# The mixer phase of a hybrid decoder step: another order of the vector and GpSimd work between two chunks, and one buffer less

## What is computed

```
q, k = rotary(q), rotary(k)                       # retention, 4 heads
o_ret = retention(q, k, v) ; o_ret *= rsqrt(mean(o_ret^2)+eps) * ret_gn * silu(gate)
kk = kr * k_k ; kk = kk / |kk|                     # RWKV-7, 8 heads of 64
kr = kr * (1 + (a - 1) * k_a)
y, S = rwkv7_scan(r, decay, kr, vr, -kk, kk * a)
y = (y - mean) * rsqrt(var + eps) * lnx_w + lnx_b
bonus = sum(r * kr * r_k, per head) * vr
y = (y + bonus) * g
```

## Time and profile before

| | |
|---|---|
| median of 3 runs | 2093.28 us (2092.87 to 2094.78) |
| the profiled execution | 2092.87 us, span 2091.0 us, 1.9 us outside the span |
| mixer phase | from about 348 us to 790 us of the span |
| its eight pairs | from about 370 us to 734 us |
| PE busy over the span | 87% |
| mean granted PE clock | 0.929 of full speed |

### The profile page before, as it was taken

How to read it: one execution, slowest core, us unless ns; L and a number is a source line. 1 busy time by engine, 2 the same in 40 slices (tenths; PEclk the granted TensorE clock), 3 DMA queues, 4 the chain that set the end, 5 groups by cost and what they waited for, 6 DMA issues and landing times. The chain is left out here.

```text
span 2091.0 us, 35611 instructions
## 1 busy us (share of the span) xinstructions
PE 1813.1 (87%) x14874; PEld 1491.2 (71%) x14874; DVE 1191.2 (57%) x1316; ACT 825.8 (39%) x930; POOL 338.3 (16%) x307
## 2 busy tenths in 40 slices
PE   7999994888888885899999998728999999999940
PEld 7998883777777764687888885326888888888830
DVE  4543101677777565514233331167999999999916
ACT  5111211333434323402121210006777777777713
POOL 1322001234433330000000000011111111111013
PEclk9999997999999887999999999858999999999975
DMA  7765216121222208553001016249999999999837
GB/s 272 241 201 176 89 48 188 46 103 71 80 76 75 83 18 293 208 209 111 31 31 62 31 51 256 97 156 343 403 403 400 404 399 407 403 402 403 326 118 305
DMA packets 111973, 419.12 MB, mean 200 GB/s; under 512 B 25892, under 2 KB 44264, under 8 KB 82920
## 3 DMA queue, kind: packets, MB, share of 16 engines
q1 hardware_dynamic: 97272, 370.80, 47.3%
q0 software_dynamic: 7072, 25.69, 3.1%
q10 hardware_dynamic: 7504, 20.78, 2.7%
HBM read 350.10 MB, written 75.53 MB: 204 GB/s over the span
## 5 line engine op out<-in xcount | busy, mean ns | idle before, releaser
L2491 DVE TENSOR_TENSOR ex_w_lo<-moe_raw,ex_w_hi 128x2048 fp32r<-128x2048 f32 x192 | 431.2, 2284 | 67.0 <-ACT ex_w_hi L2556 66.9
L2556 ACT CAST ex_w_hi<-moe_raw 128x2048 fp32r<-128x2048 f32 x192 | 364.1, 1913 | 133.3 <-PE banks L2401 90.3
L2401 PE MATMUL banks<-ex_w_hi,ex_x_hi 128*128 128x512 f32 x512 | 208.1, 406 | 10.8 <-issue 6.3
L2401 PE MATMUL banks<-ex_w_hi,ex_x_lo 128*128 128x512 f32 x512 | 202.1, 395 | 0.0
L2401 PE MATMUL banks<-ex_w_lo,ex_x_hi 128*128 128x512 f32 x512 | 201.6, 394 | 0.0
L472 PE MATMUL banks<-pj_w_hi,pj_x_hi 128*128 128x448 f32 (+1 forms) x504 | 191.4, 380 | 11.2 <-DVE pj_x_lo L303 11.2
L472 PE MATMUL banks<-pj_w_lo,pj_x_hi 128*128 128x448 f32 (+1 forms) x504 | 191.1, 379 | 0.0
L472 PE MATMUL banks<-pj_w_hi,pj_x_lo 128*128 128x448 f32 (+1 forms) x448 | 170.0, 379 | 0.0
L2401 PEld LDWEIGHTS banks<-ex_w_hi,ex_x_hi 128*128 128x128 f32 x512 | 97.5, 190 | 42.9 <-issue 21.8
L472 PEld LDWEIGHTS banks<-pj_w_hi,pj_x_hi 128*128 128x128 f32 x504 | 95.4, 189 | 25.2 <-DVE pj_x_lo L303 11.2
L2401 PEld LDWEIGHTS banks<-ex_w_hi,ex_x_lo 128*128 128x128 f32 x512 | 97.4, 190 | 21.3
(11 more groups left out here) (380 smaller groups left out, 3817.2 us busy)
## 6 DMA issues: line engine op xcount, KB each, us to landing
moe_raw<-w_e_gate SPq DMA_DIRECT2D x64, 1024.0 KB, 7.7
moe_raw<-w_e_up SPq DMA_DIRECT2D x64, 1024.0 KB, 7.6
moe_raw<-w_e_down SPq DMA_DIRECT2D x64, 1024.0 KB, 7.7
blocks<-ex_y ACTq DMA_DIRECT2D x32, 512.0 KB, 7.6
mx_pin<-proj SPq DMA_DIRECT2D x8, 1664.0 KB, 6.6
h<-at_h SPq DMA_DIRECT2D x18, 512.0 KB, 2.6
at_slots<-cache_mem_k SPq DMA_DIRECT2D x8, 1024.0 KB, 13.3
at_slots<-cache_mem_v SPq DMA_DIRECT2D x8, 1024.0 KB, 6.9
```

Of the source, the lines that this page charges most:

```text
L2401: ins = pe.matmul(out, a, b, start=first and i == 0, stop=final and i == 2)
L2491: v.tensor_tensor(w_lo[:, j], raw[:, j], as_f32(w_hi[:, j]), ALU.subtract).then_inc(S_("w_split"), 1)
L2556: act.copy(w_hi[:, j], raw[:, j]).then_inc(S_("w_high"), 1)
```

## The change

Only the order of instructions, one buffer and two waits change; no operation is added or taken away.

- DVE: `keys(j)` goes from behind level 2 to behind level 1, `key_sum(j)` from behind level 4 to behind level 2, in front of level 3. `y_sum(i - 1)` goes from level 3 to level 4. Behind level 5 the order becomes `key_norm`, `ret_out`, `att_mask`, `decay`, `state(i, 0)`, and only then `y_out(i - 1)`, then `operands(j)`, `state(i, 1)`. `bonus_sum` and `ret_gate` leave levels 1 and 2; for chunk j they now stand at the end of `pair(i)`, in front of `ret_state(j)`.
- POOL: `y_terms(i)` comes after the powers, and `ret_gain(i + 1)` after that, in front of the next `rotary`.
- `tb` has one buffer instead of two, so `y_terms(i)` waits for `y_out(i - 1)`.
- ACT: `key_square(j)` goes in front of its level 3.

```diff
-        y, yq, tb = sb("y", [P, WW]), sb("yq", [P, WW]), sb("tb", [P, 2, WW])
+        y, yq, tb = sb("y", [P, WW]), sb("yq", [P, WW]), sb("tb", [P, WW])
...
-                    v.tensor_tensor(o_w[:], y[:], tb[:, i % 2], ALU.add).then_inc(S_("o_w_ready"), 1)
+                    v.tensor_tensor(o_w[:], y[:], tb[:], ALU.add).then_inc(S_("o_w_ready"), 1)
...
                     level(i, 1)
-                    bonus_sum(i)
+                    keys(j)
                     level(i, 2)
-                    ret_gate(i)
-                    keys(j)
+                    key_sum(j)
                     level(i, 3)
                     ret_sum(i)
+                    turned_lora(j)
+                    level(i, 4)
+                    rates(j)
                     if i >= 1:
                         y_sum(i - 1)
-                    turned_lora(j)
-                    level(i, 4)
-                    key_sum(j)
-                    rates(j)
                     level(i, 5)
+                    key_norm(j)
+                    ret_out(i)
                     att_mask(j)
-                    key_norm(j)
                     decay(j)
-                    ret_out(i)
+                    state(i, 0)
                     if i >= 1:
                         y_out(i - 1)
-                    state(i, 0)
                     operands(j)
                     state(i, 1)
+                    bonus_sum(j)
+                    ret_gate(j)
...
+                ret_gate(0)
                 key_norm(0)
...
                 decay(0)
+                bonus_sum(0)
                 operands(0)
...
                 pair(NT - 1)
-                bonus_sum(NT)
-                ret_gate(NT)
...
-                    if i >= 2:
-                        po.wait_ge(S_("o_w_ready"), i - 1)
-                    g, tbi = gw[:, i % 3, :], tb[:, i % 2]
+                    if i >= 1:
+                        po.wait_ge(S_("o_w_ready"), i)
+                    g = gw[:, i % 3, :]
...
+                ret_gain(0)
                 for i in range(NT):
                     rotary(i + 1)
-                    y_terms(i)
-                    ret_gain(i)
                     ret_pow(i)
+                    key_pow(i + 1)
                     if i >= 1:
                         y_pow(i - 1)
-                    key_pow(i + 1)
-                ret_gain(NT)
+                    y_terms(i)
+                    ret_gain(i + 1)
...
                     level(i, 2)
+                    key_square(j)
                     level(i, 3)
-                    key_square(j)
                     level(i, 4)
```

More of the change, by code:

```diff
@@ L873, in y_terms @@
                     po.wait_ge(S_("gate_copied"), i + 1)
-                    if i >= 2:
-                        po.wait_ge(S_("o_w_ready"), i - 1)
-                    g, tbi = gw[:, i % 3, :], tb[:, i % 2]
-                    lk(po.tensor_tensor(heads(tbi), heads(V_in(i)), over(bonus[:, i % 2, :], WN), ALU.mult))
-                    lk(po.tensor_tensor(tbi, tbi, V_["rwkv_lnx_b"], ALU.add))
-                    lk(po.tensor_tensor(tbi, tbi, g, ALU.mult))
+                    if i >= 1:
+                        po.wait_ge(S_("o_w_ready"), i)
+                    g = gw[:, i % 3, :]
+                    lk(po.tensor_tensor(heads(tb[:]), heads(V_in(i)), over(bonus[:, i % 2, :], WN), ALU.mult))
+                    lk(po.tensor_tensor(tb[:], tb[:], V_["rwkv_lnx_b"], ALU.add))
+                    lk(po.tensor_tensor(tb[:], tb[:], g, ALU.mult))
                     po.tensor_tensor(g, g, V_["rwkv_lnx_w"], ALU.mult).then_inc(S_("tb_ready"), 1)
```

## The result

The changed kernel took 2116.28 us (median of 4 runs, 2113.14 to 2119.77) beside 2094.03 us of the kernel before (4 runs): a ratio of 1.0103, 95% interval 1.0082 to 1.0125. That is 17 to 26 us more, and the forecast was 2118. The profiled execution took 2118.49 us, 25.6 us more than that of before, with a span of 2116.7.

The account below looks back on a forecast made before the run. PE was taken as the bound, with waits that instruction order can change. Terms 1.2 + 22.2 + 0 + 3 - 6.5 - 0.5 + 6 = 25.4 us on a span of 2091.0 led to 2118 us, range 2098 to 2134.

Parts of the forecast that it names:

- The end of a pair: From `state(i, 0)` to `products`: stretched `operands` and queued DVE work make `products` 3.7 us late, 22.2 over six steps.
- the step from pair 0 to 1: First pair's end, without `y_out`: 2.7 us of new work and slower L672 against 1.98 idle cost 1.2 us.
- Level 3: PE's `hgT` waits, 6.8 us, go; `X`, 0.85 us late behind `key_sum` in eight pairs, replaces them: 0.
- The load: Chunk load waits for `tb_ready`; later `rotary` meets the `TTT` products, +3; PE's waits for `qk` vanish, -6.5.
- The clock: PE's stops around `products` bring more dips to 1.2 GHz, four over all: +6 us, bounds 0 and +14.
- The last pair and the tail: `qk` waits vanish, 6.5 in all, once 3.6; in the tail `y_out(7)` no longer runs against `y_terms(8)`, -0.5.
- (a): Rival at a pair's end: the port does not stretch `operands`, `products` 0.2 late, 2092 to 2097 us; chance 0.10.
- (b): Rival at level 3: the `hgT` wait goes and none takes its place, up to 6.8 us, 2088; chance 0.06.
- (c): Rival: every step dips, `products` and `first` at 1.2 GHz, stretch at upper bound, 2136 (2129 as worked out); chance 0.12.
- stretch of 5.0 per step: Upper bound at a pair's end: `products` 5.0 us late if all moved DVE work stretches as `operands` does.

Follow-up runs that it names:

- ten sums: Kernel before plus ten additional sums over 512 columns (6.1 us of DVE work) in front of each `ret_state`; 2121.33 us, 1.0126.
- the middle of the change alone: Kernel before with only `keys`, `key_square`, `key_sum`, `turned_lora`, `y_sum` and POOL's `key_pow` moved as in the change; 2097.45 us, 1.0023.
- `turned_lora` first: Kernel before with `turned_lora(j)` moved directly behind level 3, in front of `ret_sum` and `y_sum`; 2091.25 us, 0.9991.
- the load cut in two: Kernel before, `turned_lora` directly behind level 3, query/key columns and rotary table loaded once `rotary(i+1)` is done, other columns as before; 2081.59 us, 0.9942.

## Why the prediction was right, step by step

**The end of a pair** is confirmed in each of its terms: `operands` 1.53 to 1.76 us (about 1.7 forecast), L714 1.04, L672 1.26 (1.25), `products` late by 1.18 at `turn` and 2.94 less 0.44 at the copy, 3.68 (3.7). Over the six steps that makes 8.7 + 16.5 - 2.7 = 22.5 us, and 22.2 were forecast. In the step from pair 0 to 1 `products` is 1.42 - 0.44 = 1.0 us late at the copy instead of 1.2; from copy to copy that step grew by 1.9 us (43.05 to 44.98), half a microsecond of it by `X` of level 3 and half because the copy now begins closer to `products`. The runs with two halves of `tb`, with the bonus moved back, and with ten sums show that both causes are real: the wait that the single `tb` makes and the queue in front of `ret_state`. By the ratios the first taken away gives back 17 us of the 22, the second 4, and only the first of these is clear of the noise.

**Level 3** came out as forecast, a wait for a wait: 8.2 us for `X` against 6.8 for `hgT` and 0.4 for `X` over eight pairs.

**The load**: the load of chunk 6 is issued at 605.84, just behind `y_terms` (605.75), and `qk` is never waited for, as forecast. It gave back 2.9 us in the six steps and 3.6 in pair 7. Five of the six pairs were hit at L701 or L702, four of them at both, which stood at 928 and 943 ns instead of 692 in the mean of eight: 3.9 us in all, 3 forecast.

**The clock** was mis-sized. The term was +6 with an upper bound of 14, and PE's busy time in the six pairs rose by 13.9 us. Not all of that lengthened the path. In pairs 2 to 6 `products` took 3.1 to 3.7 us instead of 1.98; without this, PE would have waited longer for L701 and L702, which `rotary` held up. Its waits for `TTT` in the six pairs are the same before and after:

```profile
PE banks L1087 <- DVE mx_TTT L702: 11.8, 6, 2.0
```

```profile
PE banks L1087 <- DVE mx_TTT L702: 11.8, 6, 2.3
```

So 3.9 of the 13.9 us stand for that hold-up, and an estimate of the clock's own part is 13.9 - 3.9 = 10 us. The same estimate for the ten sums gives 4.3 - 4.5, nothing. That slow stretches come behind the stops is borne out: `products` took 1.98 us in pair 1, behind one stop of 1.42 us, and 3.1 to 3.7 in pairs 2 to 7, behind two, of 1.2 and 2.9 (2.7 and 1.8 in pair 4). With two halves of `tb`, behind one stop of 0.4 to 2.1 us, it took 1.98 in every pair, and with ten sums, behind one of 3.9, 2.6 to 3.5. Why almost the same lateness costs 10 us of clock in one order and nothing in the other is not shown, and this is the weakest number of the forecast.

**What hid that.** The last pair and the tail gave 4.7 and 0.9 us back, against 3.6 and 0.5. And the mixers began 3.3 us earlier (329.96 instead of 333.22, first memset), in a phase that the change does not touch: chance of the two executions, for in the thirteen profiles this lies between 328.8 and 333.2. Without it the profiled time would have been 2121.8. The sum 25.4 against 25.6 is closer than its terms, and that is luck; by the medians the change costs 22 us.

**Rivals.** (a), no stretch, is refuted by the timeline. (b), that nothing replaces the wait for `hgT`, is refuted by the middle of the change alone; and even where nothing does, with `turned_lora` first, the time does not come back. (c), the dearer clock, was half right: PE's busy time rose by its 14 us, of which some 10 lengthened the path, and its stretch of 5.0 per step did not come.

## What to carry to other kernels

Before moving work on an engine that isn't the bound, find its idle time at that very place and compare: here 1.98 us of cover took 2.7 us of new work, while many microseconds under the levels stood free. A buffer taken away does not only add a wait; it sets the moment at which the waiting engine starts, and where two engines hold each other up, as DVE and POOL do here, that moment decides what gets slower. A wait of PE that is removed is not yet time saved: look at what the next engine's data comes behind, and at the granted clock. And PE's busy time is not the clock's price by itself: a slow stretch can fill what would have been a wait.

## What the runs showed of the hardware

- Small DVE operations suffer from POOL in proportion most: scaling 128x8 numbers took 0.17 us alone and 0.78 to 0.99 beside a POOL product of 128x512, which put some 0.7 us per pair into PE's waits. The 128x256 product L672 went from 0.42 to 1.26, the 128x512 ones of `operands` from 0.68 to 1.53 to 1.76.
- In the kernel with the load cut in two, the pairs of the first profile lay at 44.3 us, with one at 44.7, although 9 us of waits were gone; PE's busy time had grown by 8.9 us to 242.4. Over the thirteen profiles PE was busy in the six pairs for 230.5 to 247.5 us on the same products, and for 233.5 and 230.5 in the two of the kernel before. It differs between orders and between executions of one order, and no run here shows what decides it.
